# GLA: each token's product with itself moved from the matmul engine to VectorE, chunk evictions placed earlier, steps of the last pair of MLA heads in another order

## The reference

```
b     = cumsum(log_f)                              # per key dimension
decay = where(causal, exp(min(b_i - b_j, 0)), 0)   # i: query, j: key
att   = einsum('ijd,jd->ij', q_i * decay, k_j)
o     = att @ v
```

## Time and profile before

| what | value |
|---|---|
| median of 3 runs | 807.15 us (806.45 to 807.23) |
| the profiled execution's own time | 807.16 us |
| its span, first to last instruction | 805.3 us |
| mean granted clock of TensorE | 0.998 of full |
| PE busy | 795.3 us (99%) |
| DVE busy | 463.8 us (58%) |
| ACT busy | 410.9 us (51%) |
| POOL busy | 126.3 us (16%) |

### The profile page before, as it was taken

One profiled execution on the slowest core, in us unless ns is written; L12 is line 12 of the kernel. 1 busy time (PEld: TensorE's weight loads), 2 busy tenths in 40 slices (PEclk: granted clock), 3 DMA queues, 4 the chain that ended last, 5 costly groups with the idle time before them and its releaser, 6 DMA issues.

```text
span 805.3 us, 11742 instructions
## 1 busy us (share of the span) xinstructions
PE 795.3 (99%) x4138; PEld 680.7 (85%) x4138; DVE 463.8 (58%) x673; ACT 410.9 (51%) x614; POOL 126.3 (16%) x215
## 2 busy tenths in 40 slices
PE   9999999999999999999999999999999999999996
PEld 7888888888888888888888888888899999978885
DVE  5566666655554454557445645455666667754554
ACT  6753544445455454564445645335556555544452
POOL 7411132112011030230000010050000000000222
PEclk9999999999999999999999999999999999999999
DMA  9874666656657666644567666566554454435612
GB/s 315 285 220 132 183 165 172 184 161 180 176 166 198 177 198 183 204 136 144 196 196 200 179 185 195 154 196 180 164 156 138 120 181 156 153 112 169 200 55 105
DMA packets 78141, 140.30 MB, mean 174 GB/s; under 512 B 9096, under 2 KB 14384, under 8 KB 77968
## 3 DMA queue, kind: packets, MB, share of 16 engines
q1 hardware_dynamic: 76496, 137.34, 57.2%
q10 hardware_dynamic: 1440, 1.84, 0.7%
q0 software_dynamic: 160, 0.52, 0.2%
HBM read 137.06 MB, written 2.62 MB: 173 GB/s over the span
## 4 chain that ended last, share of the span: by engine, by line
PE 98%; issue 1%; DVE 0%; ACT 0%; POOLq 0%; POOL 0%; ACTq 0%; DVEq 0%
PE ps L1331 24%; PE ps L1333 24%; PE ps L1332 24%; PE ps L1716 2%; PE ps L1715 2%; PE ps L1717 2%; PE ps L1353 2%; PE ps L1798 1%; PE ps L1758 1%; PE ps L1757 1%; PE ps L1759 1%; PE ps L1514 1%; PE ps L1388 1%; PE ps L1467 1%; PE ps L1769 1%
## 5 line engine op out<-in xcount | busy, mean ns | idle before, releaser
L930 DVE TENSOR_TENSOR w_lo<-raw,w_hi 128x1024 fp32r<-128x1024 f32 x239 | 302.7, 1268 | 285.8 <-ACT w_hi L607 285.2
L607 ACT ACTIVATE w_hi<-raw 128x1024 fp32r<-128x1024 f32 x236 | 249.8, 1059 | 295.5 <-PE ps L1333 280.3
L1331 PE MATMUL ps<-w_hi,a_hi 128*128 128x512 f32 x868 | 341.6, 394 | 0.2 <-issue 0.2
L1333 PE MATMUL ps<-w_hi,a_lo 128*128 128x512 f32 x868 | 338.2, 390 | 0.0
L1332 PE MATMUL ps<-w_lo,a_hi 128*128 128x512 f32 x868 | 337.9, 389 | 0.0
L1333 PEld LDWEIGHTS ps<-w_hi,a_lo 128*128 128x128 f32 x868 | 162.9, 188 | 34.4
L1331 PEld LDWEIGHTS ps<-w_hi,a_hi 128*128 128x128 f32 x868 | 163.0, 188 | 33.2 <-issue 0.6
L1332 PEld LDWEIGHTS ps<-w_lo,a_hi 128*128 128x128 f32 x868 | 163.1, 188 | 32.4
L1715 PE MATMUL ps<-a_hi,w_hi 128*128 128x256 f32 x160 | 45.8, 286 | 0.0
L1716 PE MATMUL ps<-a_hi,w_lo 128*128 128x256 f32 x160 | 45.3, 283 | 0.0
L1717 PE MATMUL ps<-a_lo,w_hi 128*128 128x256 f32 x160 | 45.3, 283 | 0.0
(11 more groups left out here) (265 smaller groups left out, 792.4 us busy)
## 6 DMA issues: line engine op xcount, KB each, us to landing
raw<-in_w_in_even SPq DMA_DIRECT2D x111, 512.0 KB, 3.8
raw<-in_w_in_odd SPq DMA_DIRECT2D x48, 512.0 KB, 3.7
raw<-in_w_out_even SPq DMA_DIRECT2D x32, 512.0 KB, 3.8
raw<-in_w_out_odd SPq DMA_DIRECT2D x32, 512.0 KB, 3.7
raw<-in_w_kv_up SPq DMA_DIRECT2D x16, 512.0 KB, 3.7
raw<-in_w_q_up SPq DMA_DIRECT2D x16, 384.0 KB, 3.3
xs<-in_x SPq DMA_DIRECT2D x6, 256.0 KB, 8.8
even<-in_final_norm SPq DMA_DIRECT2D x1, 1024.0 KB, 6.4
```

The lines of the kernel that those rows point to most:

```text
L607: return a.activation(w_hi[:, ring, 0:w], raw[:, s, 0:w], ACT.Copy)
L930: return v.tensor_tensor(w_lo[:, ring, 0:w], raw[:, s, 0:w], w_hi[:, ring, 0:w].bitcast(F32), ALU.subtract)
L1331: m.matmul(acc, a_hi[:, k, tok], hi, start=first, stop=False)
L1333: ins = m.matmul(acc, a_lo[:, k, tok], hi, start=False, stop=last)
```

## The change

1. PE's 8 products of the tiles with themselves in level 0 are gone (and `levels_done` counts two signals less), with their wait for `k_turned`, POOL's backward copy and the final causal clearing on POOL. In their place DVE multiplies the staged queries and keys elementwise (`own_tokens`) and sums them per head. For tile 1 the sums go through DRAM, written by ACT (`own_sent`) and read back by POOL with an indirect transfer in reversed order. DVE then multiplies an identity matrix with the sums, which gives `att` with its diagonal filled and zeros elsewhere (`copied(0)`).
2. In the query and key chunks, `evac` and `heads_out` of a chunk stand before step k = 7, not behind it (chunk 0 excepted).
3. In each MLA pair DVE copies `kn_t` before it makes `qr_lo`.
4. Behind the last pair: DVE's `z_prep(0)` is split around the second half of `masked`, `z_prep(1)` comes a step sooner on ACT and DVE, and `last_weighted` stands right behind `z_prep(2)`, before a piece instead of behind it.

```diff
 def levels_done(lev):
-    return lev + 2
+    return lev
@@ POOL
+            step(g.iota(rows_back[:, :], pattern=[[0, 1]], base=P - 1, channel_multiplier=-1))
...
                     g.tensor_copy(e1, b1).then_inc(gd_ready, 1)
-                    pool.wait_ge(t_free_a, freed(U_QK + 2))
-                    pool.wait_ge(t_free_d, freed(U_QK + 2))
-                    g.tensor_copy(k_both[:, ::-1], g_k[:, 512:]).then_inc(k_turned, 1)
+                    pool.wait_ge(same_written, 16)
+                    g.indirect_dma_start(same_back, None, same_turn,
+                                         bass.IndirectOffsetOnAxis(ap=rows_back[:, :], axis=0)).then_inc(same_turned, 16)
...
-            for t in range(T):
-                v = att[:, 512 * t:512 * t + 512].rearrange("p (a q) -> p a q", q=P)
-                g.affine_select(out=v, in_=v, compare_op=ALU.is_ge, fill=0.0, base=-(P - 1) * t,
-                                pattern=[[0, GH], [1, P]], channel_multiplier=2 * t - 1).then_inc(att_ready, 1)
@@ ACT
+            def own_sent():
+                act.wait_ge(same_summed, 2)
+                act.dma_start(same_turn, same[:, 1, :]).then_inc(same_written, 16)
...
-                    ahead(b, between={1: [] if par else [lambda: heads_out(c - 1)], 2: [lambda: level(lev)], 4: [lambda: level(lev + 1)]})
+                    ahead(b, between={1: [] if par else [lambda: heads_out(c - 1)], 2: ([own_sent] if c == C_SBQK else []) + [lambda: level(lev)],
+                                      4: [lambda: level(lev + 1)], 7: [chunk_out]})
...
-                {1: [lambda: z_prep(1)], 2: [lambda: weights_out(None)], 3: [lambda: z_prep(2)], 5: [lambda: z_prep(3)]},
+                {0: [lambda: z_prep(1)], 2: [lambda: weights_out(None)], 3: [lambda: z_prep(2)], 5: [lambda: z_prep(3)]},
@@ DVE
+            def own_tokens():
+                dve.wait_ge(evac_a, 2)
+                dve.wait_ge(evac_d, 2)
+                for t in range(T):
+                    v.scalar_tensor_tensor(out=att[:, 512 * t:512 * t + 512], in0=stg[0][:, t, :], scalar=SB_SCALE, in1=stg[1][:, t, :],
+                                           op0=ALU.mult, op1=ALU.mult).then_inc(same_made, 1)
+                for t in range(T):
+                    dve.wait_ge(same_made, t + 1)
+                    dst = same[:, 1, ::-1] if t else same[:, 0, :]
+                    v.tensor_reduce(dst, att[:, 512 * t:512 * t + 512].rearrange("p (h q) -> p h q", h=GH),
+                                    mybir.AxisListType.X, ALU.add).then_inc(same_summed, 1)
...
                 if lev == 0:
-                    for n, (bank, dst) in enumerate(((6, att_x), (7, att[:, 0:512]), (5, att[:, 512:1024]))):
-                        dve.wait_ge(lev_done, n + 1)
-                        v.tensor_copy(dst, ps[:, bank, :]).then_inc(lev_copied, 1)
+                    dve.wait_ge(same_summed, 2)
+                    dve.wait_ge(lev_done, 1)
+                    v.tensor_copy(att_x, ps[:, 6, :]).then_inc(lev_copied, 1)
+                    dve.wait_ge(consts, 1)
+                    dve.wait_ge(same_turned, 16)
+                    for dst, diagonal, own in ((att[:, 0:512], ident[:, :], same[:, 0, :]), (att[:, 512:], ident[:, ::-1], same_back)):
+                        v.tensor_tensor(dst.rearrange("p (h q) -> p h q", h=GH), diagonal.unsqueeze(1).to_broadcast([P, GH, P]),
+                                        own.unsqueeze(2).to_broadcast([P, GH, P]), ALU.mult).then_inc(lev_copied, 1)
...
-                evac(par, c, stg[par][:, 1, :], r1)
-                if par:
-                    heads_out(c - 1)
+                    ahead(b, between={0: [own_tokens] if c == C_SBQK else [], 1: [] if par else [lambda: heads_out(c - 1)],
+                                      2: [lambda: decayed(lev)], 3: [lambda: copied(lev)], 5: [lambda: decayed(lev + 1)], 7: [chunk_out]})
...
+                dve.wait_ge(kt_done, p + 1)
+                v.tensor_copy(kn_t, ps[:, 2, :]).then_inc(evac_d, 1)
                 dve.wait_ge(qr_taken, p + 1)
                 v.tensor_tensor(qr_lo, q_rot, qr_hi.bitcast(F32), ALU.subtract).then_inc(qr_ready, 1)
-                dve.wait_ge(kt_done, p + 1)
-                v.tensor_copy(kn_t, ps[:, 2, :]).then_inc(evac_d, 1)
...
-            masked(PAIRS - 1)
-            z_prep(0)
+            masked(PAIRS - 1, lambda: z_prep(0, (0,)))
+            z_prep(0, (1,))
...
-                {1: [lambda: z_prep(1)], 2: [lambda: weights_out(PAIRS, last=True)], 3: [lambda: z_prep(2)], 4: [last_weighted], 5: [lambda: z_prep(3)]},
+                {0: [lambda: z_prep(1)], 2: [lambda: weights_out(PAIRS, last=True)], 3: [lambda: z_prep(2), last_weighted], 5: [lambda: z_prep(3)]},
@@ PE
-                    pe.wait_ge(k_turned, 1)
-                    for t in range(T):
-                        for h in range(GH):
-                            n = (GH - 1 - h) if t else h
-                            keys = k_both[:, P * n:P * n + P] if t else g_k[:, P * h:P * h + P]
-                            ins = m.matmul(ps[:, 7 - 2 * t, P * n:P * n + P], keys, g_q[:, 512 * t + P * h:512 * t + P * h + P],
-                                           start=True, stop=True)
-                        ins.then_inc(lev_done, 1)
```

More of the change, by code:

```diff
@@ L206, in build @@
         gla_g = sb("gla_g", [P, GV])
+        same = sb("same", [P, T, GH])
+        same_turn = nc.dram_tensor("same_turn", (P, GH), F32).ap()
         v_turn = [nc.dram_tensor(f"v_turn{i}", (P, CW), F32).ap() for i in range(2)]
@@ L218, in build @@
         rstd = sb("rstd", [P, 24])
+        same_back = ssum[:, 36:40]
         idle = sb("idle", [P, 2])
@@ L244, in build @@
         gd_ready, ge_ready, gq_ready, lev_done, lev_copied = (sem(n) for n in ("gd_ready", "ge_ready", "gq_ready", "lev_done", "lev_copied"))
-        att_ready, go_done, gy_ready, gg_ready = (sem(n) for n in ("att_ready", "go_done", "gy_ready", "gg_ready"))
-        k_turned, v_written, v_turned = sem("k_turned"), sem("v_written"), sem("v_turned")
+        go_done, gy_ready, gg_ready = (sem(n) for n in ("go_done", "gy_ready", "gg_ready"))
+        v_written, v_turned = sem("v_written"), sem("v_turned")
+        same_made, same_summed, same_written, same_turned, same_set = (
+            sem(n) for n in ("same_made", "same_summed", "same_written", "same_turned", "same_set"))
         sk_ready, sz_done, sabs_ready, sexp_ready, slog_ready, ssp_ready, ssel_ready = (sem(n) for n in ("sk_ready", "sz_done", "sabs_ready", "sexp_ready", "slog_ready", "ssp_ready", "ssel_ready"))
@@ L515, in _ @@
                 two_heads(i)
-            step(g.iota(rows_back[:, :], pattern=[[0, 1]], base=P - 1, channel_multiplier=-1))
             for i in range(SBH // 2 - 2, SBH // 2):
@@ L716, in _, with chunk_out @@
                 b, par, lev = B_GQK + c, c % 2, 2 * (c - C_SBQK)
+                def chunk_out():
+                    evac(par, c, stg[par][:, 0, :], r0)
+                    if par:
+                        heads_out(c - 1)
                 if c == 0:
@@ L719, in _ @@
                 elif c == 1:
-                    ahead(b, between={2: [gates_log]})
+                    ahead(b, between={2: [gates_log], 7: [chunk_out]})
                 else:
-                    ahead(b, between={1: [] if par else [lambda: heads_out(c - 1)], 2: [lambda: level(lev)], 4: [lambda: level(lev + 1)]})
+                    ahead(b, between={1: [] if par else [lambda: heads_out(c - 1)], 2: ([own_sent] if c == C_SBQK else []) + [lambda: level(lev)],
+                                      4: [lambda: level(lev + 1)], 7: [chunk_out]})
                 if c == 0:
                     act.wait_ge(rstd_ready, 1)
-                evac(par, c, stg[par][:, 0, :], r0)
+                    chunk_out()
                 if c == 0:
@@ L1081, in _, with chunk_out @@
                 lev = 2 * (c - C_SBQK)
+                def chunk_out():
+                    evac(par, c, stg[par][:, 1, :], r1)
+                    if par:
+                        heads_out(c - 1)
                 if c == 0:
@@ L1084, in _ @@
                     dve.wait_ge(rstd_ready, 1)
+                    chunk_out()
                 elif c == 1:
-                    ahead(b, between={0: [alpha_low, gates_taken], 1: [gates_biased], 3: [log_gates], 6: [sums_taken]})
+                    ahead(b, between={0: [alpha_low, gates_taken], 1: [gates_biased], 3: [log_gates], 6: [sums_taken], 7: [chunk_out]})
                 else:
-                    ahead(b, between={1: [] if par else [lambda: heads_out(c - 1)], 2: [lambda: decayed(lev)], 3: [lambda: copied(lev)], 5: [lambda: decayed(lev + 1)]})
-                evac(par, c, stg[par][:, 1, :], r1)
-                if par:
-                    heads_out(c - 1)
+                    ahead(b, between={0: [own_tokens] if c == C_SBQK else [], 1: [] if par else [lambda: heads_out(c - 1)],
```

(7 more changed lines are left out.)

1 line of the change is left out of this document (removed).

## The result

The changed kernel took 802.96 us (median of 6 runs, 802.62 to 803.29); the kernel before took 807.10 us on the same chip (median of 6, 806.45 to 807.34). The ratio is 0.9949, with a 95% interval of 0.9939 to 0.9959. The forecast was 803.2 us.

A forecast was written before the change was run, and what follows sets the result against it. PE was taken to bound the kernel for 98%. Seven terms, 1.78 + 0.28 + 0.17 + 0.20 + 0.38 + 0.22 + 0.89 = 3.92 us, took 807.16 to 803.2 us; own range 802.6 to 803.9, 8-in-10 range 802.5 to 804.9.

The forecast's parts named there:

- the seven places: PE's path: level 0 1.78, transposes of chunks 1 and 3 0.28 and 0.17, first scores 0.20, last pair 0.38, 0.22, 0.89 us.
- part 1: Level 0: sixteen records of tokens' products with themselves leave PE, 1.78 us gained; added work on other engines costs 0.
- the first place behind the last pair: L1331 starts 0.45 us late, waiting for `z_prep(0)`; splitting it gains 0.38 us, some 0.07 remains.
- The rival that only the products go: Second signals close behind keep the waits at transposes, scores and last pair: 805.4 us, chance 20%.
- The rival of no change: New DVE work delays decays or pieces of several levels, or a landing between 84.1 and 84.7: about 807 us, chance 4%.
- two doors: Ways added work could make PE wait: `decayed(0)` before level 0, margin 1.4 us; `copied(0)` before piece 7, cost 0.
- the landing: Sums of tile 1 return for `copied(0)` between 74.1 and 80.5 us, taken as 76.5; no cost even at the upper end.
- the prediction's own sign of being right: On the DMA queues: the small transfers of the sums land within 6.6 us in sum.
- Parts 2 to 4: Earlier evictions gain 0.28 and 0.17 us, keys before queries 0.20, reordering behind the last pair 0.38, 0.22 and 0.89.
- `z_prep(3)`: Behind the last pair: next to be late, needs 3.2 us of PE's 3.5, so 0.3 us left and no wait.
- The last `z_step`: Behind the last pair on PE: start near 719.3 us (723.20 - 3.92) as a sign of being right.
- The late return: DVE waits in `copied(0)` for the indirect read, piece 7 is late, one for one beyond 80.5: 809.5 us, chance 5%.

The follow-up runs named there:

- The parts undone: Changed kernel with old order restored: evictions 803.53 us; keys 803.63; steps behind last pair 804.48; last weighting only 803.96; all but the products of tokens with themselves 805.47.
- two steps later: Changed kernel with ACT's write of the sums (`own_sent`) moved two steps later: 804.59 us, ratio 0.9969.
- the kernel with three loops: Changed kernel with the elementwise products and sums of `own_tokens` made three times over: 806.72 us, ratio 0.9994.
- one step later: Changed kernel with ACT's write of the sums (`own_sent`) moved one step later: 803.08 us, ratio 0.9951.
- the four extra products: Changed kernel with four extra DVE products of 128x512, both inputs in SBUF, ahead of `copied(0)`: 802.58 us.
- two loops: Changed kernel with the elementwise products and sums of `own_tokens` made twice: 803.01 us, ratio 0.9946.

## Why the prediction was right

**The bound and the reading.** PE is in order and never has a choice, so the seven places are separate terms that add up. That was assumed. The parts undone show it, on top of part 1: each brings back its own waits and no other, to 0.01 us in their profiles, and to 0.03 at the first place behind the last pair (0.325 against 0.355). The rival that only the products go (20%, 805.4) needed a second releaser close behind the first. Only the first wait behind the last pair comes near to it, with 0.355 gained of 0.45, and that part was in the sum. The rival of no change (4%) needed delays at several levels or a landing beyond 84; neither came.

**Part 1.** The 1.78 us came as 1.787. Its two doors held. The first has a margin of 1.7 us now: 2.5 us more work ahead of the decays made no wait, 5.0 us did. At the second, the landing was mis-sized: taken as 76.5, it was 78.4. Two errors partly cancel in that, and that they did is luck. I priced a write of 2 KB near the 2.1 us of the smallest row and it took 4.4, so the way back took 9.6 us where 6.6 was taken, and the prediction's own sign of being right, landings within 6.6 us in sum, failed (4.4 + 4.9 = 9.3). But ACT issued the write 1.1 us sooner than thought. That it cost nothing rests on the slack of 2.1 us at piece 7; the range from both sides, up to 10.6, did hold it.

**Parts 2 to 4.** All to within 0.03 us. `z_prep(3)`, named as next to be late with 0.3 us left, makes no wait.

**What the sum left out.** The restart behind each wait, 0.21 us in all. It fits the 0.2 us by which the time came out below the forecast, but the runs of the changed kernel lie 0.7 us apart, so the times can't show it; the profiles do. The last `z_step` starts at 718.90 us and not at the 719.3 given: the restarts and the 0.13 of the opening make most of that.

**The late return (5%, 809.5).** The mechanism is real: two steps later it makes PE wait, at the place and nearly from the landing that were given. One for one, it would have needed a landing near 84, 5.6 us later than measured, to make the kernel slower than before. The rival's price of one us for each us of delay is the weak step, though: the kernel with three loops shows a wait of 2.4 us that cost 4.2, as much as the whole gain. If the clock falls so at piece 7 too, which no run shows, a landing some 4 us later than measured would do.

## What to carry to other kernels

Read a wait as the distance between two starts, less the same distance where nothing waits, and add a restart of 0.03 to 0.07 us (0.11 behind the wait of 1.30); the idle column showed 0.16 us less than the last wait was. Before work is put ahead of a deadline on another engine, add up its idle time and its margin there (2.5 us here) and keep within it, because beyond it the price need not stay one for one: at 2.4 us of waiting the clock fell too, in the profile and, by their times, in most runs. Don't price a round trip through DRAM by its bytes: here it took 9.6 us for 2 KB, and the write 4.2 to 4.8 beside the loads of weights against 1.4 on nearly idle queues. Give it a range, and check that its upper end still costs nothing.

## What was not expected of the hardware

- The 2 KB write took 4.2 to 4.8 us in most of these kernels, beside 512 KB loads of weights, and 1.4 us in the two where the queues were nearly idle then (DMA share 0.05 and 0.06). The indirect read of 2 KB took 2.5 us with empty queues (share 0.02) and 4.9 at a share of 0.65; with one step later it also took 2.5, at a share of 0.48, beside the four extra products 4.2, at 0.81, with two loops 5.8, at 0.87, and with three loops 7.5, at 0.80. The share alone doesn't set it.
- DVE and POOL slowed each other down, not always both. DVE's product took 1.30 us instead of 0.69 beside POOL's L484, which kept its 1.07 us there (1.06 with DVE idle). L484 took 1.51 beside the four extra products, and the same operation in the kernel before, L478, took 2.04 beside a piece of DVE.
- The granted clock fell after a wait of 2.44 us, and not after one of 1.30, in one profile each.
